# Three re-orderings in a three-block model kernel: mLSTM head work a piece later, expert one-hots a piece sooner, weight halves ahead of the last taps

## The reference, cut to what matters

```python
# first block: mLSTM mixer
q, k, v, o, gates = split(x @ w_in)              # 4 heads, chunks of 128 tokens
log_f = log_sigmoid(gates[..., 4:] + b)          # then cumulative sum and running maximum
qk  = einsum(q, k) * exp(d - m_t)                # decays, per head
h   = num / maximum(abs(den), exp(-m_t))         # per head and chunk
h   = rms_norm(h, head_norm)
out = (sigmoid(o) * h) @ w_out
# second block: experts, 8 heads x 16 of 16384
act  = einsum('td,thkd->thk', x, u_tab[eidx])
hact = gelu(act) * softmax(top scores)
out  = einsum('thk,thkd->td', hact, v_tab[eidx])
# third block: last feed-forward net
up = x @ w_up                                    # 2 x 3072
up = causal_dwconv(up, conv_f_w, conv_f_b)       # 3 taps
gate, val = split(up)
x = x + rms_norm((gelu(gate) * val) @ w_down)
```

## Time and profile before

| what | value |
|---|---|
| time of the kernel, median of 3 runs | 2957.06 us (2956.54 to 2959.25) |
| profiled execution, its own time | 2958.24 us |
| its span, first to last instruction | 2956.4 us |
| mean granted TensorE clock | 0.989 |
| TensorE busy | 2867.6 us, 97% of the span |
| VectorE busy | 1951.0 us, 66% |
| ScalarE busy | 1633.7 us, 55% |
| chain that ended last: TensorE's share | 89% |

### The profile page before, as it was taken

One profiled execution on the slowest core, in us unless ns is written; L12 is line 12 of the kernel. 1 busy time (PEld: TensorE's weight loads), 2 busy tenths in 40 slices (PEclk: granted clock), 3 DMA queues, 4 the chain that ended last, 5 costly groups with the idle time before them and its releaser, 6 DMA issues.

```text
span 2956.4 us, 44425 instructions
## 1 busy us (share of the span) xinstructions
PE 2867.6 (97%) x17894; PEld 2564.7 (87%) x17894; DVE 1951.0 (66%) x3360; ACT 1633.7 (55%) x2792; POOL 338.7 (11%) x309
## 2 busy tenths in 40 slices
PE   7999999899999999999999999999999999999998
PEld 6878888688878877799898999999888889989997
DVE  5656665676576656758764898777555566756774
ACT  5544554665556555456554444777455555645663
POOL 0000000000010002000000344896000000000000
PEclk9999999999999999999999999999999999999999
DMA  5544456356434544345346454334555564536453
GB/s 193 203 160 150 160 193 226 121 177 218 164 114 150 203 178 161 128 145 175 93 129 200 167 180 168 129 136 147 193 195 194 190 238 127 161 95 209 135 201 128
DMA packets 304220, 490.33 MB, mean 166 GB/s; under 512 B 10816, under 2 KB 236480, under 8 KB 295312
## 3 DMA queue, kind: packets, MB, share of 16 engines
q1 hardware_dynamic: 302880, 480.09, 48.1%
q0 software_dynamic: 1136, 7.41, 0.7%
HBM read 485.36 MB, written 2.10 MB: 165 GB/s over the span
## 4 chain that ended last, share of the span: by engine, by line
PE 89%; DVE 6%; ACT 3%; issue 1%; DMA 1%; POOL 0%; SPq 0%; DVEq 0%; POOLq 0%; ACTq 0%
PE ps L591 30%; PE ps L521 11%; PE ps L525 10%; PE ps L522 10%; PE ps L670 10%; PE ps L669 5%; PE ps L542 3%; PE ps L1100 2%; DVE halves L1342 2%; PE ps L1135 1%; ACT XX L2550 1%; DVE XX L1380 1%; ACT halves L2525 1%; PE ps L1155 1%; DVE AR L2172 1%
## 5 line engine op out<-in xcount | busy, mean ns | idle before, releaser
L2525 ACT ACTIVATE halves<-raw 128x1024 fp32r<-128x1024 f32 (+1 forms) x843 | 879.0, 1051 | 717.1 <-PE ps L591 341.3
L1342 DVE TENSOR_TENSOR halves<-raw,halves 128x1024 fp32r<-128x1024 f32 (+1 forms) x807 | 965.2, 1217 | 232.5 <-ACT halves L2525 229.8
L521 PE MATMUL ps<-XX,halves 128*128 128x256 f32 (+1 forms) x2360 | 591.0, 288 | 0.0
L522 PE MATMUL ps<-XX,halves 128*128 128x256 f32 (+1 forms) x2360 | 582.3, 285 | 0.0
L591 PE MATMUL ps<-halves,XX 128*128 128x512 f32 x2256 | 526.4, 394 | 9.1 <-ACT XX L2550 6.3
L591 PEld LDWEIGHTS ps<-halves,XX 128*128 128x128 f32 x2256 | 425.8, 190 | 103.7 <-issue 11.7
L521 PEld LDWEIGHTS ps<-XX,halves 128*128 128x128 f32 (+1 forms) x2360 | 455.1, 193 | 2.6 <-issue 2.0
L522 PEld LDWEIGHTS ps<-XX,halves 128*128 128x128 f32 (+1 forms) x2360 | 456.3, 193 | 0.1
L525 PE MATMUL ps<-XX,halves 128*128 128x256 f32 (+1 forms) x2360 | 333.1, 284 | 0.7 <-DVE halves L1342 0.7
L591 PE MATMUL ps<-halves,R 128*128 128x512 f32 x1416 | 327.0, 393 | 3.7 <-DVE halves L1342 1.9
L670 PE MATMUL ps<-XX,halves 128*128 128x512 f32 x1264 | 319.2, 394 | 4.9 <-DVE XX L1380 4.9
(11 more groups left out here) (368 smaller groups left out, 3516.8 us busy)
## 6 DMA issues: line engine op xcount, KB each, us to landing
raw<-in_w_ffn_in SPq DMA_DIRECT2D x88, 1024.0 KB, 5.1
raw<-in_w_in SPq DMA_DIRECT2D x74, 1024.0 KB, 5.2
raw<-in_uT SPq DMA_DIRECT2D x64, 1024.0 KB, 4.8
raw<-in_peer_v SPq DMA_DIRECT2D x64, 1024.0 KB, 4.9
raw<-in_w_ffn_out SPq DMA_DIRECT2D x44, 1024.0 KB, 4.8
raw<-in_w_up SPq DMA_DIRECT2D x24, 1024.0 KB, 5.7
raw<-in_mlstm_w_in SPq DMA_DIRECT2D x12, 1024.0 KB, 5.2
raw<-in_w_down SPq DMA_DIRECT2D x12, 1024.0 KB, 4.8
```

What stands on the lines that cost most here:

```text
L521: mm(o[:, ts], hi[:, q, 0:M], xh[:, k0 + q, ts], start=first and q == 0, stop=False)
L522: mm(o[:, ts], hi[:, q, 0:M], xl[:, k0 + q, ts], start=False, stop=False)
L1342: te.tensor_tensor(lo, src, hi.bitcast(F32), ALU.subtract).then_inc(k.lo_made, 1)
L2525: act(hi, src, ACT.Copy).then_inc(k.hi_made, 1)
```

## The change

Four edits of order; no arithmetic changes.

1. mLSTM, rows: on VectorE `gates` and `decays` become one side list from the first piece of k on, two steps a piece instead of four.
2. mLSTM, heads and turns: the side list of `heads` starts one piece later on all three engines (`later(6, ...)`), and the turns, products and halves of `ml.y` 0 and 2 stand between the sixth and seventh pieces of o; those of 4 and 6 stay behind the last.
3. Experts: ScalarE and VectorE make group 0's one-hots at piece 73 (`hot_at`). TensorE's `weigh` stays where it was.
4. Last net: in the rounds f = 24 and 26 ScalarE and VectorE make the halves of coming `w_down` pieces ahead of the last pairs' work: low halves to `cur+4`, then `cur+5`; high halves to `cur+5`, then `cur+6`.

```diff
+def later(n, side):
+    for _ in range(n):
+        yield
+    yield from side
...
+def hot_at(n):
+    return (0,) if n == FIRST_HOT - 1 else [g for g in groups_of(n) if g]
... TensorE, mlstm
-        pe.begin(heads(8, (values, nothing, nothing, nothing)), 6)
-        features("ml.o", 8, X, rx)
+        pe.begin(later(6, heads(8, (values, nothing, nothing, nothing))), 6)
+        features("ml.o", 6, X, rx)
+        turn_y(0)
+        turn_y(2)
+        features("ml.o", 8, X, rx, start=6)
         pe.finish()
-        for c in range(0, 8, 2):
+        turn_y(4)
+        turn_y(6)
... VectorE, mlstm
         def decays():
-            for _ in range(4):
+            yield from gates()
+            for _ in range(2):
                 yield
...
-        v.begin(gates(), 4)
+        v.begin(decays(), 2)
         features(nothing, "ml.k", 4)
-        v.finish()
-        v.begin(decays(), 2)
         tokens(value, 1024)
         v.finish()
-        v.begin(heads(8, (nothing, divide, nothing, normal)), 6)
-        features(nothing, "ml.o", 8)
+        v.begin(later(6, heads(8, (nothing, divide, nothing, normal))), 6)
+        features(nothing, "ml.o", 6)
+        for y in (gated_y, low_y):
+            y(0)
+            y(2)
+        features(nothing, "ml.o", 2)
         v.finish()
+        for y in (gated_y, low_y):
+            y(4)
+            y(6)
... VectorE, peer (ScalarE the same, its first wait moves to n == FIRST_HOT - 1)
-            for g in groups_of(n):
+            for g in hot_at(n):
                 hot(g)
... VectorE, ffn3
+            if f >= 24:
+                low_to(v.cur + 4 + (f - 24) // 2)
             if f >= 4:
                 low(f - 4)
... ScalarE, mlstm
-        a.begin(heads(8, (values, divide, nothing, nothing)), 6)
-        features(out_of("ml.o", oT, ACT.Sigmoid), "ml.o", 8)
+        a.begin(later(6, heads(8, (values, divide, nothing, nothing))), 6)
+        features(out_of("ml.o", oT, ACT.Sigmoid), "ml.o", 6)
+        high_y(0)
+        high_y(2)
+        features(out_of("ml.o", oT, ACT.Sigmoid), "ml.o", 8, first=6)
         a.finish()
+        high_y(4)
+        high_y(6)
... ScalarE, ffn3
+            if f == 26:
+                high_to(a.cur + 6)
             if f >= 4:
                 high(f - 4)
+            if f == 24:
+                high_to(a.cur + 5)
             if 2 <= f < 26:
                 gate(f - 2)
```

More of the change, by code:

```diff
@@ L777, in mlstm, with turn_y @@
         pe.finish()
-        pe.begin(heads(8, (values, nothing, nothing, nothing)), 6)
-        features("ml.o", 8, X, rx)
-        pe.finish()
-        for c in range(0, 8, 2):
+        def turn_y(c):
             b = main.take(pe, ("ml.y", c))
@@ L788, in mlstm @@
             filled(("ml.y", c), ins)
+        pe.begin(later(6, heads(8, (values, nothing, nothing, nothing))), 6)
[3 more added lines that the diff above has]
+        features("ml.o", 8, X, rx, start=6)
+        pe.finish()
+        turn_y(4)
+        turn_y(6)
         down("ml", 8, k.pair(14336, 8), out_halves("ml"))
@@ L1675, in mlstm, with gated_y, low_y @@
         te.memset(vx[:, :, :, 256:257], 1.0).then_inc(*step.mark("ml.ones"))
-        v.begin(gates(), 4)
+        v.begin(decays(), 2)
         features(nothing, "ml.k", 4)
-        v.finish()
-        v.begin(decays(), 2)
         tokens(value, 1024)
         v.finish()
-        v.begin(heads(8, (nothing, divide, nothing, normal)), 6)
-        features(nothing, "ml.o", 8)
-        v.finish()
[L1685 to L1697, removed]
+        def gated_y(c):
+            b = main.of(("ml.y", c))
+            v.wait_ge(*full["ml.y", c])
+            v.wait_ge(*main.gone(("ml.o", c)))
+            for cc_ in range(2):
+                ins = te.scalar_tensor_tensor(tmp[:, c + cc_, :], ps[:, b, cc_ * 256:cc_ * 256 + 256],
+                                              col("hn", c + cc_), oT[:, c + cc_, :], ALU.mult, ALU.mult)
+            ins.then_inc(*main.done(("ml.y", c)))
+        def low_y(c):
+            v.wait_ge(*s["out_hi"].need(("ml", c)))
+            low_half(ymT[1][:, c:c + 2, :], tmp[:, c:c + 2, :], ymT[0][:, c:c + 2, :]) \
+                .then_inc(*s["out_lo"].mark(("ml", c)))
+        v.begin(later(6, heads(8, (nothing, divide, nothing, normal))), 6)
[4 more added lines that the diff above has]
+        features(nothing, "ml.o", 2)
+        v.finish()
+        for y in (gated_y, low_y):
+            y(4)
+            y(6)
         down("ml", 8, True, 1.0)
@@ L2613, in split, with features @@
         act(k.by_tokens(key, 0), ps[:, main.of((key, "t", 0)), :], ACT.Copy).then_inc(*main.done((key, "t", 0)))
-    def features(evac, key, nf, KT=8, by_four=False):
+    def features(evac, key, nf, KT=8, by_four=False, first=0):
         if by_four:
@@ L2619, in features @@
             split(key)
-        for f in range(4 if by_four else 0, nf):
+        for f in range(4 if by_four else first, nf):
             for q in range(1 if KT == 8 else 2):
@@ L2769, in mlstm, with high_y @@
         a.finish()
-        a.begin(heads(8, (values, divide, nothing, nothing)), 6)
-        features(out_of("ml.o", oT, ACT.Sigmoid), "ml.o", 8)
-        a.finish()
-        for c in range(0, 8, 2):
+        def high_y(c):
             a.wait_ge(*main.gone(("ml.y", c)))
             act(ymT[0][:, c:c + 2, :], tmp[:, c:c + 2, :], ACT.Copy).then_inc(*s["out_hi"].mark(("ml", c)))
+        a.begin(later(6, heads(8, (values, divide, nothing, nothing))), 6)
[3 more added lines that the diff above has]
+        features(out_of("ml.o", oT, ACT.Sigmoid), "ml.o", 8, first=6)
+        a.finish()
+        high_y(4)
+        high_y(6)
         down("ml", 8, True, 1.0)
@@ L3090, in peer @@
                 act(w, w, ACT.Exp).then_inc(*s["act"].mark("pr.exp"))
-            if n == FIRST_HOT:
+            if n == FIRST_HOT - 1:
                 a.wait_ge(*aux.gone(("pr", "sel", 1)))
```

## The result

| | before | after |
|---|---|---|
| median (18 runs each) | 2955.49 us (2950.43 to 2962.39) | 2950.12 us (2948.63 to 2952.97) |
| ratio, 95% interval | | 0.9983 [0.9976, 0.9990] |
| profiled execution: time, span, mean clock | 2958.24, 2956.4, 0.989 | 2948.63, 2946.8, 0.991 |

The changed kernel is 5.4 us faster by the medians; the interval reaches from 3.0 to 7.1 us. The prediction said 2950.8. That is more than the medians differ by: the profiled execution of the changed kernel is the fastest of its 18 runs, and the one of before is 2.8 us slower than before's median.

The account below looks back on a forecast made before the run. TensorE, busy 97% of the span, was taken as the bound, so only its waits and clock counted. Terms of -2.2 (mLSTM), -1.4 (experts) and -3.85 (last net) made -7.4 from 2958.24: 2950.8 us, range 2947.5 to 2954.8.

Parts of the forecast that it names:

- The rows: mLSTM gates' rows: four low halves ahead of the last row make TensorE's turn 1.1 us later, with a 3 us wait.
- The clock behind it, one drop kept: Behind the wait for the gates' rows: one stretch at 1.2 GHz stays at the same price, adding nothing to the sum.
- Rival A: mLSTM: the low clock lasts twice as long, costing 1.7 us, so 2952.5; chance 0.22.
- Heads and turns: mLSTM: idles before the first `values` and before the first down product go, gaining 1.5 and 1.8 us.
- The cover of 0.9 us at the last `normal`: mLSTM turns: VectorE's last two `normal` are done 0.9 us before TensorE wants them.
- Experts: Before `weigh` of group 0: one-hots start earlier on ScalarE, gaining 1.4 of TensorE's 2.3 us idle.
- the tie at group 1: Experts: group 1's one-hots end near 1851.9 and TensorE wants them at 1852.0, so no loss was counted.
- Last net: w_down products: earlier low halves remove a 2.1 us wait and the 1.75 us clock drop behind it, 3.85 in all.
- rival B: Last net: the clock drop was that execution's own, absent from the median; gain 5.7 in all, 2951.4; chance 0.20.
- The sum: Whole kernel: 7.4 us off the profile's 2958.24 gives 2950.8, 6.3 under the median; this main forecast had chance 0.45.
- The case: Whole kernel: chances of 0.53 for faster by over 0.2% (5.9 us), 0.44 for same, 0.03 for slower.
- Rival D: mLSTM gates' rows: a late high half lengthens TensorE's wait; over 11 us late, the whole gain is gone; chance 0.03.

Follow-up runs that it names:

- e2: The kernel before with only the edit of the gates' rows (two steps a piece); 2959.26 us against 2956.49, ratio 1.0006.
- e3: The changed kernel with the gates' side list at three steps a piece, finished before the decays start; 2945.76 us, ratio to before 0.9965.
- e6: The changed kernel with the rows' edit undone, so only heads and turns of the mLSTM are changed; 2948.42 us, ratio to before 0.9974.
- e1: The kernel before with only the edit of the last net; 2951.63 us against 2956.49, ratio 0.9987.
- e7: The kernel before, unedited, profiled once more; 2958.72 us.
- e4: The changed kernel with the decays' side list one piece later on TensorE, ScalarE and VectorE; 2945.65 us, ratio to before 0.9964.
- e5: The changed kernel with the decays a piece later and group 0's one-hots ahead of piece 76's high half on ScalarE; 2943.65 us against before's 2956.96.
- e8: The changed kernel with gates at three steps a piece, decays a piece later and first one-hots ahead of piece 76's high half; 2942.66 us, ratio to before 0.9952.

## Why the prediction was right, point by point

- **The rows, +1.1.** Right in sign and size: +1.14 (15.17 against 14.03), with a wait of 2.81 where about 3 was expected; e2 shows it alone, and e3 that the low halves in the list set it. This edit cost time on its own: before turned the rows after 14.03, and e6, without it, starts the down product 1.13 us sooner than the changed kernel.
- **The clock behind it, one drop kept.** Right for the changed kernel's profile (0.51 from 253.3 to 256.7). Rival A is real too: 6.8 us in e2. The prediction made too little of it: it names one stretch of 6.8 us, but the trace of before has five of them beside seven of 3.4. Whether the clock drops here at all went with the waits in every profile: the six with 1.1 us or more of idle in v's pieces ahead of the turn (before, e1, e6, e7, the changed kernel, e2) have a drop, the four with 0.5 or less (e3, e4, e5, e8) have none.
- **Heads and turns, -1.5 and -1.8.** The mechanism held, the size was low: -3.75, not -3.3 (60.36 from the turn of the rows to the down product before, 56.61 after; 56.62 in e6). The mis-sized term is the idle in brackets. It runs from the modelled end of the last product, and in the rows products overlap: 24 of them are 5.71 us long, but at the pace of 0.2267 the next could start after 5.44. TensorE before:

```profile
270.79 5.71 PE L591 MATMUL ps<-halves,XX 128*128 128x512 f32 x24
...
306.27 1.91 PE L786 MATMUL ps<-ident,AR 128*128 128x128 f32 x16
```

By the pace the loss ahead of the first `values` was 277.98 - (270.79 + 24 x 0.2267) = 1.75, not 1.47. Eight turns take 0.79 us (300.58 to 301.37 and 307.20 to 307.99), so 16 from 306.27 end at 307.85, and the loss at the down product was 2.09, not 1.76.
- **The cover of 0.9 us at the last `normal`.** It held, by 1.3: VectorE ended them at 305.93 and TensorE's last turns start at 307.20.
- **Experts, -1.4.** 2.27 to 0.83, and the tie at group 1 held. e5 took the rest by stepping over the transfer's wait.
- **Last net, -3.85.** -3.84 between the profiles: 2.20 for the wait and 1.64 for a clock drop that not every execution has. e2 and e7 have the same wait and no drop, 67.67. So "with no wait there is no drop" held, but the reverse, a drop behind that wait in every run, did not. The first half of rival B is shown: the drop was that execution's own. Whether the median run of before lacked it is not. I gave B 0.20 and the case with the drop 0.45; three profiles of that wait show the drop once.
- **The sum.** Its level came out better than its parts, and that is in part luck. The forecast was 2950.8 and the median 2950.12. But the sum took 7.4 off the profiled execution of before, 6.3 off the three runs' median, and the 18 runs give 5.4, with an interval from 3.0 to 7.1: a smaller gain, counted from a median of before that is 1.6 lower than that of the three. Rival B's gain of 5.7 is nearer the 5.4, but the interval holds 5.7 and 6.3 both; it does not reach 7.4. The touched places gave 7.9 between the profiles, and 6.25 without the last net's drop.
- **The case.** I gave 0.53 to a gain of over 0.2% and 0.44 to less. It was 0.17%, with an interval from 0.10 to 0.24, so by the point the less likely case came. I also said that a difference under 0.2% could hardly be told from none: with 18 runs each it can.
- **Rival D** has no support: the rows never waited for a high half.

What stays open: why the clock falls behind one wait and not behind the same wait in another execution. The runs show that it differs, not what decides. How often each drop comes is not measured either; three profiles are too few. No run has the experts' edit alone: its 1.4 us stand on the waits in the traces.

The experiments point to a better version, and e5 is it: 2943.65, 13.3 us under before measured beside it (ratio 0.9956 [0.9942, 0.9970]), against 0.9983 [0.9976, 0.9990] for the change. e8 is as fast, with one edit more.

## What to carry to other kernels

Spreading a serial chain of small operations between the halves that feed TensorE is paid for at the chain's end: count what stands ahead of its last link, not only what the chain delays. When an engine waits, ask what it could do meanwhile: here a consumer moved one piece later took away 4.3 us where making the producer faster took 3.8, and the two did not add. Price a lost stretch by the pace of the work around it, not by the idle in brackets. And before a clock drop goes into a sum, profile the same kernel again: the one in the last net came in one execution of three.

## What the runs showed of the hardware

- A wait of 1.91 us on TensorE, with the same code around it, was followed by 3.4 us at 1.2 GHz in one execution (69.31 us for the 288 products) and by none in two others (67.67 in e7, the same kernel, and in e2). Waits of 1.4 to 1.8 us on TensorE in the mLSTM (before, e1, e2, e7) had a granted clock of 1.00 behind them each time.
- Behind the same wait of 2.8 us and the same small products the clock was low for 3.4 us in the changed kernel, from 1.9 us behind the wait, and for 6.8 us in e2, from 0.5 us behind it. The Trainium skill (TensorE: Matmul & The Clock Gate, Part 1: The HAM clock gate) says that the monitor's window runs free of the kernel's start; these runs fit that, since the places of the low clock differ between the two executions of before (2889.7 in the first, 1848.9 in e7).
- VectorE's low half of a 128x1024 piece is 1.22 us long in the timeline, but the next instruction starts 1.14 us after it does (2.27 us for two, e3 against the changed kernel).
